# Moving the block sums of x to the bottom of the on-chip memory, and splitting the last down products of two groups into halves of 256 columns

## The reference

```python
x = x + 0.5 * swiglu(rms_norm(x, g), w_gate, w_up, w_down)   # (silu(h@w_gate) * (h@w_up)) @ w_down
x = x + mixer(rms_norm(x, g))                                # layer 0: RG-LRU + block attention
x = x + 0.5 * swiglu(...)                                    # layer 1: convolution + top-k attention
```

## Time and profile before

| | before |
|---|---|
| median of 3 runs | 1911.82 us |
| the profiled execution | 1911.45 us |
| its span, first to last instruction | 1909.7 us |
| TensorE matmul busy | 1879.0 us (98%) |
| VectorE busy | 1460.6 us (76%) |
| ScalarE busy | 1021.5 us (53%) |
| matmuls | 11902 |
| granted TensorE clock, mean | 0.998 |

### The profile page before, as it was taken

The page is one execution under the profiler, slowest core; times in us unless marked ns, Lnnn a source line. Parts: engine busy times, 40 slices in busy tenths (PEclk is TensorE's granted clock), DMA queues, the critical chain, the costliest instruction groups (busy, mean ns, idle before and its releaser), DMA issues.

```text
span 1909.7 us, 31417 instructions
## 1 busy us (share of the span) xinstructions
PE 1879.0 (98%) x11902; PEld 1671.6 (88%) x11902; DVE 1460.6 (76%) x2330; ACT 1021.5 (53%) x1640; POOL 194.7 (10%) x251
## 2 busy tenths in 40 slices
PE   7999999999999999999999999999999999999999
PEld 6899899888778899898889989877778789899997
DVE  8879587577779788597877859756989878687684
ACT  7546264477776355364645526455456766364451
POOL 1311010000001011010011101011111001011000
PEclk9999999999999999999999999999999999999999
DMA  7666661211136565463465646166765376565441
GB/s 242 153 199 183 177 168 60 99 67 67 58 109 180 167 171 138 151 176 108 132 168 156 155 139 182 45 163 158 171 152 132 86 199 173 154 182 160 131 114 66
DMA packets 94789, 271.66 MB, mean 142 GB/s; under 512 B 10504, under 2 KB 10760, under 8 KB 94640
## 3 DMA queue, kind: packets, MB, share of 16 engines
q1 hardware_dynamic: 63456, 201.22, 30.6%
q0 software_dynamic: 29232, 64.50, 19.4%
q10 hardware_dynamic: 1952, 3.93, 1.0%
HBM read 223.07 MB, written 2.77 MB: 118 GB/s over the span
## 4 chain that ended last, share of the span: by engine, by line
PE 88%; DVE 7%; ACT 3%; issue 2%; DMA 0%; DVEq 0%; ACTq 0%
PE ps_unit L804 13%; PE ps_unit L806 13%; PE ps_unit L805 13%; PE ps_y L868 6%; PE ps_y L870 6%; PE ps_y L869 6%; PE ps_s L868 4%; PE ps_t L868 4%; PE ps_t L870 4%; PE ps_t L869 4%; PE ps_s L869 4%; PE ps_s L870 4%; PE ps_s L804 1%; DVE cv L2464 1%; PE ps_s L805 1%
## 5 line engine op out<-in xcount | busy, mean ns | idle before, releaser
L1405 ACT ACTIVATE gw_hi<-gu 128x512 fp32r<-128x512 f32 (+1 forms) x400 | 318.9, 799 | 151.0 <-PE ps_s L870 69.4
L1939 DVE TENSOR_TENSOR gw_lo<-gu,gw_hi 128x512 fp32r<-128x512 f32 (+1 forms) x400 | 354.6, 901 | 49.0 <-ACT gw_hi L1405 36.2
L804 PE MATMUL ps_unit<-a_hi,w_hi 128*128 128x512 f32 x892 | 351.2, 394 | 5.9 <-DVE w_lo L1867 3.2
L805 PE MATMUL ps_unit<-a_lo,w_hi 128*128 128x512 f32 x892 | 347.8, 390 | 0.0
L806 PE MATMUL ps_unit<-a_hi,w_lo 128*128 128x512 f32 x845 | 329.2, 390 | 0.0
L1340 ACT ACTIVATE w_hi<-raw 128x1024 fp32r<-128x1024 f32 (+1 forms) x125 | 125.3, 1003 | 305.6 <-PE ps_unit L806 301.8
L804 PEld LDWEIGHTS ps_unit<-a_hi,w_hi 128*128 128x128 f32 x892 | 167.7, 188 | 44.6 <-DVE w_lo L1867 5.4
L2076 DVE TENSOR_TENSOR t<-ps_unit,half 128x512 f32<-128x512 f32 x96 | 66.4, 691 | 173.0 <-PE ps_unit L806 172.6
L805 PEld LDWEIGHTS ps_unit<-a_lo,w_hi 128*128 128x128 f32 x892 | 167.7, 188 | 33.0
L806 PEld LDWEIGHTS ps_unit<-a_hi,w_lo 128*128 128x128 f32 x845 | 158.7, 188 | 33.7
L870 PE MATMUL ps_y<-xu_hi,gw_lo 128*128 128x256 f32 x640 | 180.3, 282 | 0.0
(11 more groups left out here) (326 smaller groups left out, 4663.8 us busy)
## 6 DMA issues: line engine op xcount, KB each, us to landing
gu<-gu_stream_dram SPq DMA_DIRECT2D x176, 512.0 KB, 5.0
raw<-w_stream_dram SPq DMA_DIRECT2D x136, 512.0 KB, 3.3
gu<-gu_stream_dram SPq DMA_DIRECT2D x80, 256.0 KB, 3.0
gu<-gu_stream_dram POOLq DMA_DIRECT2D x80, 256.0 KB, 4.2
gu<-gu POOLq DMA_DIRECT2D x80, 256.0 KB, 3.3
w_lo<-raw POOLq DMA_DIRECT2D x28, 512.0 KB, 5.0
raw<-w_stream_dram SPq DMA_DIRECT2D x32, 384.0 KB, 3.5
w_lo_3rd<-raw POOLq DMA_DIRECT2D x15, 512.0 KB, 5.5
```

The lines of the kernel that those rows point to most:

```text
L804: pe.matmul(ps, lhs_hi, rhs_hi, start=first, stop=False)
L805: pe.matmul(ps, lhs_hi, rhs_lo, start=False, stop=False)
L1405: act.activation(gw_hi[:, w, :], src, ACT.Copy).then_inc(gw_hi_done, 1)
L1939: dve.tensor_tensor(gw_lo[:, w, :], src, gw_hi[:, w, :].bitcast(F32), ALU.subtract).then_inc(gw_lo_done, 1)
```

## The change

The block sums xu_hi and xu_lo become the first tiles in the memory, ahead of xt; all tiles from xt on lie 24,576 bytes higher, gw_lo now ends where xu_lo ended. The mixer tiles that lay over xu move down with it, so that they share its new place; their order is the same but for c_pad0, which stays above. And in the first two groups of each network, the last down unit runs its last two steps as matmuls of 256 columns, two for one, on the same weights and into the same bank.

```diff
+HALVED = 2
...
+        low = top[0]
+        xu_hi = sb("xu_hi", [P, PAIRS, 3 * TH], F32R)
+        xu_lo = sb("xu_lo", [P, PAIRS, 3 * TH], F32R)
+        low_top = top[0]
         xt = sb("xt", [P, KT * T])
...
         gw_lo = sb("gw_lo", [P, 7, PIECE], F32R)
-        xu_hi = sb("xu_hi", [P, PAIRS, 3 * TH], F32R)
-        xu_lo = sb("xu_lo", [P, PAIRS, 3 * TH], F32R)
         ffn_top = top[0]
...
         bdr_hi = sb("bdr_hi", [P, 2, 4, P], F32R)
+        even_top = top[0]
+        top[0] = low
         bdr_lo = sb("bdr_lo", [P, 2, 4, P], F32R)
         xc_hi = sb("xc_hi", [P, T], F32R)
...
-        isc = sb("isc", [P, P * (2 + 3 + 4)])[:, :]
         top8 = sb("top8", [P, 8])[:, :]
         wi = sb("wi", [P, TT * HEADS])[:, :]
+        c_pad = [sb("c_pad0", [P, T + DW_TAPS - 1])[:, :]]
+        odd_top = top[0]
+        top[0] = low
+        isc = sb("isc", [P, P * (2 + 3 + 4)])[:, :]
         relu = [probs[:, 0, :], probs[:, 1, :]]
-        c_pad = [sb(f"c_pad{j}", [P, T + DW_TAPS - 1])[:, :] for j in range(4)]
+        c_pad += [sb(f"c_pad{j}", [P, T + DW_TAPS - 1])[:, :] for j in range(1, 4)]
...
+            def down_halves(i, u, ks):
+
+                g, s = u // KT, (UNIT_BASE[i] + u) % 2
+                for k in ks:
+                    hi, lo, w = of_a(1, GROUP_AT[g])(k), of_a(0, GROUP_AT[g])(k), slice(k * P, (k + 1) * P)
+                    for lhs, rhs in ((w_hi, hi), (w_hi, lo), (w_lo, hi)):
+                        for h in (slice(0, TH), slice(TH, T)):
+                            mm = pe.matmul(ps_unit[:, s, h], lhs[:, s, w], rhs[:, h], start=False, stop=True, skip_group_check=True)
+                return mm
+
             def down_unit(i, u):
 
+                tiles = GROUPS[u // KT]
                 start_unit(UNIT_BASE[i] + u, is_first=UNIT_BASE[i] + u < 2)
-                down_part(i, u, range(GROUPS[u // KT])).then_inc(unit_done, 1)
+                if u % KT < KT - 1 or u + 1 == FFN_UNITS:
+                    down_part(i, u, range(tiles)).then_inc(unit_done, 1)
+                else:
+                    down_part(i, u, range(tiles - HALVED), nk=tiles - HALVED)
+                    down_halves(i, u, range(tiles - HALVED, tiles)).then_inc(unit_done, 1)
```

More of the change, by code:

```diff
@@ L286, in build @@
         even_more = [acc[:, :], sb("row_3", [P, T])[:, :]]
-        even_top = top[0]
+        assert top[0] <= low_top
         bd_raw = sb("bd_raw", [P, UNIT], at=bd_at)[:, :]
@@ L304, in build @@
         squares = [c[:, 0:T] for c in c_pad]
-        odd_top = top[0]
+        assert top[0] <= low_top
         assert max(even_top, odd_top, ffn_top) <= nc.sbuf_usable_end, (even_top, odd_top, ffn_top)
@@ L980, in gate_right, with down_part @@
                 gu_product(block_bank(f % 2, 2), 6, *of_u(1, 1), False)
-            def down_part(i, u, ks):
+            def down_part(i, u, ks, nk=None):
                 g, n = u // KT, UNIT_BASE[i] + u
-                return blocks(n % 2, ks, of_a(1, GROUP_AT[g]), of_a(0, GROUP_AT[g]), nk=GROUPS[g],
+                return blocks(n % 2, ks, of_a(1, GROUP_AT[g]), of_a(0, GROUP_AT[g]), nk=nk or GROUPS[g],
                               wait=lambda k: pe.wait_ge(a_lo_done, FFN_BASE[i] + GROUP_AT[g] + k + 1))
+            def down_halves(i, u, ks):
[6 more added lines that the diff above has]
+                return mm
             def down_unit(i, u):
+                tiles = GROUPS[u // KT]
                 start_unit(UNIT_BASE[i] + u, is_first=UNIT_BASE[i] + u < 2)
-                down_part(i, u, range(GROUPS[u // KT])).then_inc(unit_done, 1)
+                if u % KT < KT - 1 or u + 1 == FFN_UNITS:
[3 more added lines that the diff above has]
+                    down_halves(i, u, range(tiles - HALVED, tiles)).then_inc(unit_done, 1)
             def ffn(i):
```

## The result

The changed kernel takes 1916.28 us (median of 12 runs, 1915.59 to 1917.58) beside 1911.93 us for the kernel before on the same chip (12 runs): a ratio of 1.0024, with an interval from 1.0016 to 1.0032. It is slower by 4.35 us, where 19 us less were forecast. The profiled execution has a span of 1913.9 us, 4.2 us above the span before.

A forecast was written before the change was run, and what follows sets the result against it. TensorE's matmuls were taken as the bound. 19.8 us gained on sum products less 0.6 for the halves gives 19.2 off 1911.45, so 1892.2, plus 0.37 for the median: 1892.6 us, range 1890 to 1896.

The forecast's parts named there:

- The bound: Whole kernel: TensorE is busy for 98% of the span at full clock, so only its matmuls' length or number matters much.
- Block sums at x's offset: Sum products on gw: each comes down to x's quick 1.36 us; 4.96 us a network, 19.8 us for four.
- The halves: End of the down unit: 256-column matmuls cost 0.6 us in all; x starts behind them at 1.38 us, as behind a sum.
- The slow level is not broken: Second and third groups: halves run at 113 ns and products stay at 1.41 us throughout; 1913.8 us; chance 0.12.
- The place matters: Block sums: the rival said their place has nothing to do with it, leaving only the halves' 0.6 us; 1912.4 us; chance 0.04.
- high addresses: Weights now in the highest region: if that region costs, every product takes 1.44 us; 1935 us; chance 0.05.
- VectorE stays behind: Middle tiles: VectorE could do 9.37 us against TensorE's new 9.52, its gate wait falling to some 0.16; counted as nothing.

The follow-up runs named there:

- the kernel cut at 240: The changed kernel with its split matmuls cut into 240 and 272 columns in place of 256 and 256: 1892.62 us (ratio 0.9901).
- the cut at 224: The changed kernel with its split matmuls cut at 224 columns instead of 256: 1892.88 us.

## Why the prediction was wrong

*The bound.* Right: TensorE is busy for 98%, and the difference lies in its matmuls.

*Block sums at x's offset.* Right in what it does: a sum product becomes as fast as an x product, 1.36 us where x is quick. The first groups gain 0.95 us a network, against 0.96 worked out. The reason was right too (the distance, not the region or the tile's step), with 128 bytes in place of 256 or 512.

*The halves.* Their price was right (119 ns, 0.6 us). What failed is the sentence "So I take it that x starts behind the halves as it starts behind a sum, at 1.38." It carried the second and third groups: 78.25 to 76.2 us forecast, 79.15 measured, a miss of 2.95 × 8 = 23.6 us, where forecast and result are 23.7 apart. The inference ran: a slow product on gw with an even distance ends the slow level; the halves have an even distance and are slow; so they end it too. The kernel with twelve extra matmuls shows that even ones on gw do end it; the kernels with 12 and 24 halves show that even ones on w do not. The trace before showed only one kind of matmul that ends it, and I carried over what it shared with the halves and passed over what it didn't, the tiles first of all.

*What the move took away.* This is where the loss comes from. In each tile of the kernel before, the badly placed sum products were slow themselves and, by running, put x back on the quick level: a tile took 9.76 us. With the sums well placed nothing resets it, and all seven products run at 1.413: 9.89 us. I had seen that and left it to the halves.

*The rival that came true.* "The slow level is not broken" has the outcome and the side, and 1913.8 as its time. Its condition did not come true: it supposed halves at 113 ns, and they ran at 119 and still left the level alone. So the time is near in part by luck. It was 2.5 us short: its tile was 9.87, by readings rounded to 1.41, where the sum over a group gives 9.89, which makes +1.4 us over the eight groups, and it counted nothing for the halves' 0.6; the 0.5 left is within what two executions differ by. Its chance of 0.12 was too low: "it doesn't outlast one sum product" spoke for the sums on gw, and not for the halves.

*The others.* The place matters, and high addresses cost nothing. VectorE stays behind: in the kernel cut at 240 the tile is down to the forecast 9.52 us, and it still waits for the gate, 0.32 us where 0.16 were worked out:

```profile
153.50 0.69 DVE L2011 TENSOR_TENSOR t<-sqb,ps_t 128x512 f32<-128x512 f32 x1 [0.32 <-PE ps_t L879]
...
163.02 0.69 DVE L2011 TENSOR_TENSOR t<-sqb,ps_s 128x512 f32<-128x512 f32 x1 [0.32 <-PE ps_s L879]
```

So the 19.8 us were there to be had: three ways of leaving the slow level give 1892.6 (uneven parts) and 1892.5 (twice, less the insertions).

*What stays open.* Why uneven parts on w end the slow level while even ones don't, and why six are too few. The runs show that it isn't the place of the second part (224 and 256 are both even), and that more even ones don't help; they don't show what the level is. The expectation for the cut at 224 has a reason (unequal parts shift the loads of the weights against the moving operand). Its time came true, 1893 and 1892.88, but no run tests the reason. Whether a pause lowers the level is open too: the traces have three pauses within a quick stretch, and the level fell behind 0.60 and 0.44 us, but was back at 1.36 one product behind 0.22 us (in the kernel without halves, at 71.63 us).

## What to carry to other kernels

Before a slow operation is taken away, ask what else it does by running: here it was what kept its neighbours quick, and its removal cost more than it gave. When a step is to stand in for another, list what the two share and what they don't; if the trace has only one example, the forecast hangs on whichever property was picked, and the rival that picks another deserves a like chance. And judge a change of level over a whole group, from start to start: durations alone (277, 280, 282 ns) hid two speeds that differ by 4%.

## What the runs showed of the hardware

- Matmuls of the same shape have lasting speeds. 256 columns at a distance of 64 modulo 128 bytes from their weights run at 113 ns or at 118 ns for tens of microseconds, with the clock granted in full, by what ran ahead of them. Three 512-column or twelve 256-column matmuls on the same weights tile switched to the quick one in all eight groups, and so did twelve uneven ones on another; 12 or 24 even ones on that other tile did not.
- For 256 columns the distance of the moving tile from the weights tile matters modulo 128 bytes: a shift of gw, and of the other tiles behind `stage`, by 64 bytes makes 1933.51 of 1915.97 us.
- The level can also fall within a stretch, behind a pause of 0.60 or 0.44 us, and in two traces the first network's first group was at 118 ns behind the plain tiles (gw shifted by 128 bytes: to its end; cut at 224: for half of it), where the changed kernel has 113. At 224 it rose to the quick level behind two 512-column matmuls on other tiles (onehot on relb, at 56.12 and 56.55 us); the same two didn't raise it with gw shifted by 128. A version that leaves the slow level once, ahead of a group, is not proof against such falls.
